# Expert layer: the first 128 of 512 tokens by gathered expert rows on VectorE, the other 384 by dense products

## Chip, cores and metric

One core of one Trainium2 chip runs one program, launched once. The metric is the device time of that program in microseconds; less is better. All times here are of the kernel before.

## What is computed

Two transformer blocks over 512 tokens of width 1024. The first block has attention in several forms and then a layer of product-key experts (`peer`); the second, twice, has other mixers and a gated MLP. Only the experts are touched:

```python
def peer(hn, w_q, subkeys, u, v):                    # 8 heads, 128 keys, top 16, 16384 experts
    q = (xt @ w_q).reshape(T, H, 2, 64)
    s = jnp.einsum('thcd,cnd->thcn', q, subkeys)
    s1, i1 = lax.top_k(s[:, :, 0], K)
    s2, i2 = lax.top_k(s[:, :, 1], K)
    cand = (s1[..., :, None] + s2[..., None, :]).reshape(T, H, K * K)
    sc, ci = lax.top_k(cand, K)
    e1 = jnp.take_along_axis(i1, ci // K, axis=-1)
    e2 = jnp.take_along_axis(i2, ci % K, axis=-1)
    idx = e1 * 128 + e2
    g = jax.nn.softmax(sc, axis=-1)
    a = jnp.einsum('cd,chkd->chk', xc, u[ic])        # for each chunk of tokens
    act = jax.nn.gelu(a) * gc
    return jnp.einsum('chk,chkd->cd', act, v[ic])
```

Each token takes 8 x 16 = 128 of 16384 experts, each a row of 1024 numbers in `u` and in `v`.

## The kernel before

All activations lie transposed: 128 features on the partitions, 8 such chunks, 512 tokens along the free dimension. The experts run dense: all 16384 hidden values of every token are computed, and those not chosen get weight 0. Expert (i, j) is row j of chunk i, so 128 chunks of 128 experts stand for all.

Products are made from halves: every fp32 operand is split into a rounded high part (fp32r) and the rest (low part), and each product is three matmuls, high x high, high x low, low x high. `Stream` brings the weights in pieces of 128x1024 (512 KiB), the same for all stages: `load` on SP's queue into 4 raw buffers, `high` on ScalarE (L363) and `low` on VectorE (L371) into 3 buffers each; `high` of piece n waits until TensorE has used piece n - 3 (`used`). The order on each engine's queue is that of the program text, and engines meet by semaphores.

The experts have four stages, one after the other:

- `queries`: the normalised tokens (h_hi, h_lo) and the queries.
- `expert_choice`, 48 steps. In each, TensorE computes one chunk of `a` (`Hidden.product`, L399: 8 feature chunks x 3 matmuls with 512 columns), ScalarE takes its gelu (L407), SP stores it to memory (`a_dram`). Beside it VectorE chooses for four tiles of 128 tokens: the 16 best of 128 keys for each of 16 half-heads (`sixteen`: max, match_replace and max_index of 8 at a time), all 256 sums of a head, the 16 best of those, then the names of the experts by comparisons with a range. The `low` splits have to be put between these operations by hand: `Pace` counts estimated us and lets one `low` through every 4.5.
- `expert_weights`, 80 steps, the other 80 chunks of `a`, 512 tokens in quads of 4. For each token ScalarE builds a one-hot row of the first key (L648, L651), VectorE two weighted rows of the second (L674, the share's high and low part), and TensorE multiplies them (L705, 256 columns), giving the token's 128x128 weights in two halves; VectorE adds the halves out of PSUM (`take`, L685) into `built`, which SP stores in tiles of 64 tokens (4 MiB). 128 quads are spread over the first 72 steps.
- `expert_outputs`, 128 steps. SP loads the `v` piece, a chunk of hidden values (256 KiB) and, for 4 chunks at once, the weights (1 MiB in rows of 1 KiB). VectorE multiplies them (`weigh`, L812), ScalarE and VectorE split the product (L792, L818), and TensorE accumulates 8 x 3 matmuls of 512 columns (L847) in all eight PSUM banks through the whole stage. `Angles` prepares tables for the second block on VectorE and ScalarE. At the end VectorE adds the banks to x (L836).

The two loops that set TensorE's work in the last two stages:

```python
for k in range(DC):                                       # L394, product of a chunk
    hi, lo = hi_w[:, k * P:(k + 1) * P], lo_w[:, k * P:(k + 1) * P]
    for m, (a, b) in enumerate(((hi, self.h_hi), (hi, self.h_lo), (lo, self.h_hi))):
        mm = self.nc.tensor.matmul(self.ps[n % 2], a, b[:, k, :], ...)
```

GpSimd does nothing in these stages, and no transfer in the kernel is issued from its queue.

## Time and profile before

| | |
|---|---|
| median of 3 runs | 4273.8 us (4264.1 to 4284.9) |
| profiled execution, its span | 4269.6 us |
| TensorE busy | 4059.4 us, 95% |
| VectorE busy | 2362.1 us, 55% |
| ScalarE busy | 1504.6 us, 35% |
| GpSimd busy | 85.6 us, 2% |
| moved by DMA | 497.2 MB, 116 GB/s on average |

The profiled execution's own time is known by its span, from its first to its last instruction; the median of the runs is 4.2 us above it. PE is TensorE's matmuls and PEld its weight loads, DVE VectorE, ACT ScalarE, POOL GpSimd, SP the engine that issues the transfers. Busy times are of instructions from start to end; matmuls overlap in the pipeline, so the pace of matmuls is read from their starts, not from their durations. The names of tiles are those of the program, with the stage before them (`outputs_prod`); `experts_ps` is PSUM in all expert stages.

### The profile page before, as it was taken

To read this page: it belongs to the slowest core of one execution; us is meant where nothing else is said; L and a number is where in the kernel's file an instruction comes from. 1 tells how busy PE (TensorE), PEld (TensorE's weight loads), DVE (VectorE), ACT (ScalarE), POOL (GpSimd) and SP (SyncE) were. 2 spreads that over 40 slices of the span, in tenths; PEclk is the share of its full clock that TensorE was granted. 3 is DMA by queue.
4 is the path that set the end of the run, shared out by engine and by line. 5 is a ranking of instruction groups with operands and counts; after the bars stand their busy time and mean duration, and the time that the engine had idled before them with its cause. 6 is when DMAs were issued, how large, how long until landed. Compare 5 with 4: busy or idle time off the path is not lost. (4 is left out here: it accounts for less than half of the span.)

```text
span 4269.6 us, 47277 instructions
## 1 busy us (share of the span) xinstructions
PE 4059.4 (95%) x18056; PEld 3239.5 (76%) x18056; DVE 2362.1 (55%) x4095; ACT 1504.6 (35%) x2600; POOL 85.6 (2%) x65
## 2 busy tenths in 40 slices
PE   8999999999999999999999998899998998998998
PEld 6667777788888878888887766777886766776886
DVE  3454445799899954544444356555434346565433
ACT  3222324233777742322222322333222232243221
POOL 0010000000000000000000001000000001000000
PEclk9988899999999999999999989999999989999999
DMA  3211113344555566666663222332332322242332
GB/s 125 77 60 30 38 40 116 100 141 133 165 205 190 177 245 196 190 193 188 189 195 101 85 69 70 95 125 84 94 90 74 97 60 72 77 148 74 94 89 69
DMA packets 183363, 497.15 MB, mean 116 GB/s; under 512 B 17826, under 2 KB 51268, under 8 KB 182116
## 3 DMA queue, kind: packets, MB, share of 16 engines
q1 hardware_dynamic: 183140, 494.14, 36.7%
q8 instruction: 145, 2.38, 0.2%
q14 instruction: 78, 0.64, 0.1%
HBM read 407.56 MB, written 85.98 MB: 116 GB/s over the span
## 5 line engine op out<-in xcount | busy, mean ns | idle before, releaser
L371 DVE TENSOR_TENSOR stream_lo<-stream_raw,stream_hi 128x1024 fp32r<-128x1024 f32 (+1 forms) x615 | 745.6, 1212 | 748.5 <-ACT stream_hi L363 747.1
L363 ACT ACTIVATE stream_hi<-stream_raw 128x1024 fp32r<-128x1024 f32 (+1 forms) x615 | 642.8, 1046 | 1430.5 <-PE experts_ps L847 492.0
L847 PE MATMUL experts_ps<-outputs_a_hi,stream_lo 128*128 128x512 f32 x1024 | 404.2, 395 | 0.0
L399 PE MATMUL experts_ps<-h_hi,stream_hi 128*128 128x512 f32 x1024 | 402.1, 393 | 1.5 <-PEq L100 1.5
L847 PE MATMUL experts_ps<-outputs_a_hi,stream_hi 128*128 128x512 f32 x1024 | 398.3, 389 | 4.2 <-DVE outputs_a_lo L818 4.2
L399 PE MATMUL experts_ps<-h_hi,stream_lo 128*128 128x512 f32 x1024 | 402.3, 393 | 0.0
L847 PE MATMUL experts_ps<-outputs_a_lo,stream_hi 128*128 128x512 f32 x1024 | 402.1, 393 | 0.0
L399 PE MATMUL experts_ps<-h_lo,stream_hi 128*128 128x512 f32 x1024 | 401.8, 392 | 0.0
L2334 PE MATMUL ffn_ps<-h_hi,stream_hi 128*128 128x512 f32 x704 | 287.4, 408 | 25.3 <-DVE h_lo L2371 25.3
L2334 PE MATMUL mid_ps<-h_hi,stream_hi 128*128 128x512 f32 x672 | 288.2, 429 | 24.0 <-DVE h_lo L2371 20.8
L2336 PE MATMUL ffn_ps<-h_hi,stream_lo 128*128 128x512 f32 x704 | 279.4, 397 | 0.0
L2335 PE MATMUL ffn_ps<-h_lo,stream_hi 128*128 128x512 f32 x704 | 279.4, 397 | 0.0
L2335 PE MATMUL mid_ps<-h_lo,stream_hi 128*128 128x512 f32 x672 | 271.1, 403 | 0.0
L2336 PE MATMUL mid_ps<-h_hi,stream_lo 128*128 128x512 f32 x672 | 270.3, 402 | 0.0
L847 PEld LDWEIGHTS experts_ps<-outputs_a_hi,stream_hi 128*128 128x128 f32 x1024 | 192.6, 188 | 47.5 <-issue 4.6
L847 PEld LDWEIGHTS experts_ps<-outputs_a_lo,stream_hi 128*128 128x128 f32 x1024 | 192.7, 188 | 45.1
L399 PEld LDWEIGHTS experts_ps<-h_hi,stream_lo 128*128 128x128 f32 x1024 | 192.9, 188 | 41.7
L399 PEld LDWEIGHTS experts_ps<-h_hi,stream_hi 128*128 128x128 f32 x1024 | 193.1, 189 | 41.4 <-issue 2.0
L399 PEld LDWEIGHTS experts_ps<-h_lo,stream_hi 128*128 128x128 f32 x1024 | 193.0, 188 | 39.6
L847 PEld LDWEIGHTS experts_ps<-outputs_a_hi,stream_lo 128*128 128x128 f32 x1024 | 193.1, 189 | 38.4
L674 DVE SCALAR_TENSOR_TENSOR weights_hot<-shared_sb,chosen,weights_g 128x256 fp32r<-128x256 f32 x512 | 208.5, 478 | 0.0
L407 ACT ACTIVATE experts_gelu<-experts_ps 128x512 f32<-128x512 f32 x128 | 76.5, 598 | 309.8 <-PE experts_ps L399 309.8
(439 smaller groups left out, 7146.3 us busy)
## 6 DMA issues: line engine op xcount, KB each, us to landing
stream_raw<-u SPq DMA_DIRECT2D x128, 512.0 KB, 3.9
stream_raw<-v SPq DMA_DIRECT2D x128, 512.0 KB, 4.1
stream_raw<-l_gu SPq DMA_DIRECT2D x88, 512.0 KB, 3.5
expert_hidden<-experts_gelu SPq DMA_DIRECT2D x128, 256.0 KB, 4.2
expert_weights<-built SPq DMA_DIRECT2D x8, 4096.0 KB, 14.2
built<-expert_weights SPq DMA_DIRECT2D x32, 1024.0 KB, 7.8
built<-expert_hidden SPq DMA_DIRECT2D x128, 256.0 KB, 4.1
stream_raw<-l_gate SPq DMA_DIRECT2D x48, 512.0 KB, 3.9
```

What stands on the lines that cost most here:

```text
L363: self.nc.scalar.activation(self.hi[n % self.RING][:, 0:w], self.raw[n % self.RAW][:, 0:w], ACT.Copy).then_inc(self.hi_done, 1)
L371: self.nc.vector.tensor_tensor(self.lo[n % self.RING][:, 0:w], self.raw[n % self.RAW][:, 0:w], self.hi[n % self.RING][:, 0:w].bitcast(F32) ...
L399: mm = self.nc.tensor.matmul(self.ps[n % 2], a, b[:, k, :], start=(k == 0 and m == 0), stop=(k == DC - 1 and m == 2))
L407: self.nc.scalar.activation(self.gelu[n % self.PLACES][:, :], self.ps[n % 2], ACT.Gelu_apprx_tanh).then_inc(self.gelu_done, 1)
L674: ins = V.scalar_tensor_tensor(out=hot2[quad % RING][:, k, :, :], in0=C.iota.unsqueeze(1).to_broadcast(both), scalar=chosen[:, 1, t:t + 1] ...
L847: mm = nc.tensor.matmul(ps[d], v, a[b % RING][:, :], start=(b == 0 and m == 0), stop=(b == KEYS - 1 and m == 2))
L2334: nc.tensor.matmul(out, hi, x_hi, start=first, stop=False)
L2335: nc.tensor.matmul(out, hi, x_lo, start=False, stop=False)
L2336: return nc.tensor.matmul(out, lo, x_hi, start=False, stop=last)
```

## The change

The first 128 tokens leave the dense path. `DIRECT` = 128 and `DENSE` = 384: the hidden products, the outputs' matmuls, their splits, products and stores are 384 columns wide. For tile 0 of the choice the experts' row numbers and shares stay with the tokens on the partitions (`Direct.at`, `Direct.share`). For each of a token's 128 experts (slots), GpSimd issues an indirect DMA that gathers one row of `u` for each of the 128 tokens (512 KiB) into one of 6 buffers, and VectorE computes the 128 dots in one instruction, a multiplication with its sum; after a gelu over all slots the same is done with `v`: a weighted sum, into two accumulators in turn. 36 dots lie in the weights stage, 92 dots and 128 weighted sums in the outputs, spread over 122 steps. At the end the accumulators are added, turned by eight transposes into PSUM beside the dense columns, and added to x by the same instructions as now.

The choice gets 72 steps and the weights 56. The candidates of a head are 112 instead of 256: all 16 second keys for the 4 best first keys, and 4 second keys for the other 12; the places are decoded with more bit operations (`places`). `Pace` lets a split through every 3.26. Turning a tile waits for later tiles by one, and tile 0 is not turned.

In the weights, a token's two halves are accumulated in PSUM by two matmuls of 128 columns instead of one of 256, so that a quad fits one bank (6 places instead of 3); the copy out of PSUM is made by ScalarE for even quads and by VectorE for odd ones. Weight tiles are 32 tokens wide and are loaded for 8 chunks at once. In the queries, eight transposes and two copies bring tile 0's normalised tokens onto the partitions. `Angles` runs earlier, from step 2. The host gives `u` once more, in rows.

```diff
 
-EG = 4
-WT = 64
-WTT = SEQ // WT
+DIRECT, DENSE = P, SEQ - P
+EG = 8
+WT = 32
+WTT = DENSE // WT
 GROUPS = KEYS // EG
...
 
-CHOICE_STEPS = 48
...
+        self.nc, self.u_rows, self.v_rows = nc, u_rows, v_rows
+        self.rows = [st.sb(f"rows{s}", [P, D]) for s in range(self.RING)]
+        self.tokens = st.sb("tokens", [P, D])
+        self.sums = []
+        self.at, self.share = st.sb("slot_at", [P, self.SLOTS], U32), st.sb("slot_share", [P, self.SLOTS])
+        self.dots = st.sb("slot_dots", [P, self.SLOTS])
...
+    def gather(self, pool, n):
+        source = self.u_rows if n < self.SLOTS else self.v_rows
+        if n >= self.RING:
+            pool.wait_ge(self.row_done, n - self.RING + 1)
+        j = n % self.SLOTS
+        self.nc.gpsimd.indirect_dma_start(self.rows[n % self.RING][:, :], None, source,
+                                          bass.IndirectOffsetOnAxis(ap=self.at[:, j:j + 1], axis=0)
+                                          ).then_inc(self.landed[n % self.RING], 16)
+
+    def row(self, dve, n):
+        dve.wait_ge(self.landed[n % self.RING], 16 * (n // self.RING + 1))
+        return self.rows[n % self.RING][:, :]
+
+    def dot(self, dve, j):
+        row = self.row(dve, j)
+        self.nc.vector.scalar_tensor_tensor(out=row, in0=row, scalar=1.0, in1=self.tokens[:, :], op0=ALU.mult, op1=ALU.mult,
+                                            accum_out=self.dots[:, j:j + 1]).then_inc(self.row_done, 1)
+
+    def activate(self, act):
+        act.wait_ge(self.row_done, self.SLOTS)
+        self.nc.scalar.activation(self.dots[:, :], self.dots[:, :], ACT.Gelu_apprx_tanh).then_inc(self.gelu_done, 1)
+
+    def mix(self, dve, j):
+        n, V, to, weight = self.SLOTS + j, self.nc.vector, self.sums[j % 2][:, :], self.dots[:, j:j + 1]
+        if j == 0:
+            dve.wait_ge(self.gelu_done, 1)
+            V.tensor_tensor(self.dots[:, :], self.dots[:, :], self.share[:, :], ALU.mult).then_inc(self.weight_done, 1)
+            dve.wait_ge(self.weight_done, 1)
+        row = self.row(dve, n)
+        if j < 2:
+            V.tensor_scalar(to, row, weight, None, ALU.mult).then_inc(self.row_done, 1)
+            return
+        dve.wait_ge(self.row_done, n - 1)
+        V.scalar_tensor_tensor(out=to, in0=row, scalar=weight, in1=to, op0=ALU.mult, op1=ALU.add).then_inc(self.row_done, 1)
+
+    def total(self, dve):
+        dve.wait_ge(self.row_done, 2 * self.SLOTS)
+        self.nc.vector.tensor_tensor(self.sums[0][:, :], self.sums[0][:, :], self.sums[1][:, :], ALU.add).then_inc(self.summed, 1)
...
+DOTS_EARLY = 36
...
+                def sums(first, last, width):
+                    shape = [P, HEADS, last - first, width]
+                    start = 0 if first == 0 else WIDE * TOPK
+                    to = cand[:, :, start:start + (last - first) * width].rearrange("p h (i j) -> p h i j", j=width)
+                    steps.mark(V.tensor_tensor(to, best[:, 0:HEADS, first:last].unsqueeze(3).to_broadcast(shape),
+                                               best[:, HEADS:H2, 0:width].unsqueeze(2).to_broadcast(shape), ALU.add))
+                    pace.spend(0.65)
...
                     dve.wait_ge(copied, t + 1)
-                    sixteen(H2, sc[t % 2], sc2, best, at, 0.2)
+                    sixteen(H2, sc[t % 2], sc2, best, at, 0.28)
                     V.tensor_copy(at_f[:, :, :], at[:, :, :]).then_inc(sc_free, 1)
-                    if t >= 1:
...
-                    wide = [P, HEADS, TOPK, TOPK]
-                    steps.after(V.tensor_tensor(cand[:, :, :].rearrange("p h (i j) -> p h i j", i=TOPK),
-                                                best[:, 0:HEADS, :].unsqueeze(3).to_broadcast(wide),
...
                         pace.spend(2.3)
                         steps.after(V.tensor_reduce(found_of(t, side), picked[:, :, :, :], AX_X, ALU.add))
                         pace.spend(2.3)
+                    if t == 0:
+                        V.scalar_tensor_tensor(out=direct.at[:, :], in0=found[0][:, 0, :], scalar=float(KEYS), in1=found[0][:, 1, :],
+                                               op0=ALU.mult, op1=ALU.add).then_inc(direct.named, 1)
...
         hot1 = [st.sb(f"hot1_{b}", [P, QUAD, KEYS], F32R) for b in range(RING)]
         hot2 = [st.sb(f"hot2_{b}", [P, QUAD, 2, KEYS], F32R) for b in range(RING)]
-        minus_done, g_hi_done, g_lo_done, far_done, hot1_done, hot2_done, mm_done, taken = (
-            st.sem(x) for x in ("minus_done", "g_hi_done", "g_lo_done", "far_done", "hot1_done", "hot2_done", "mm_done", "taken"))
+        minus_done, g_hi_done, g_lo_done, far_done, hot1_done, hot2_done, mm_done, taken_s, taken_v = (
...
             return range(*done)
 
+        def dots(n):
+            done = [DOTS_EARLY * (step - first) // (last - first) for step in (n, n + 1)]
...
+                def take(quad):
+                    wait_home(act, quad)
+                    act.wait_ge(mm_done, quad + 1)
+                    nc.scalar.activation(home(quad), place(quad), ACT.Copy).then_inc(taken_s, 1)
...
+                    for quad in quads(n - 1):
+                        if quad % 2 == 0:
+                            take(quad)
                     for quad in quads(n):
...
+                for n in range(Direct.RING, Direct.RING + DOTS_EARLY):
+                    direct.gather(pool, n)
 
             @block.vector
...
+                    wait_home(dve, quad)
                     dve.wait_ge(mm_done, quad + 1)
-                    V.tensor_reduce(built[tt % BUILT][:, :, at:at + QUAD].rearrange("p e t -> p t e"),
-                                    place(quad).rearrange("p t s e -> p t e s"), AX_X, ALU.add).then_inc(taken, 1)
+                    V.tensor_copy(home(quad), place(quad)).then_inc(taken_v, 1)
 
...
+                    for j in dots(n):
+                        direct.dot(dve, j)
 
             @block.tensor
...
                         for k in range(QUAD):
-                            mm = nc.tensor.matmul(place(quad)[:, k, :, :], hot1[quad % RING][:, k, :], hot2[quad % RING][:, k, :, :],
-                                                  start=True, stop=True)
+                            for part in range(2):
+                                mm = nc.tensor.matmul(place(quad)[:, k, :], hot1[quad % RING][:, k, :], hot2[quad % RING][:, k, part, :],
+                                                      start=(part == 0), stop=(part == 1))
                         mm.then_inc(mm_done, 1)
 
...
         self.w_dram, self.a_dram, self.hidden = w_dram, a_dram, hidden
-        place = flat(built[:, :, :])
+        place = built[:, :, :, :].rearrange("p b e t -> p (b e t)")
         width = WTT * EG * WT
         self.wgt = [place[:, s * width:(s + 1) * width].rearrange("p (t m) -> p t m", t=WTT) for s in range(self.W_RING)]
         rest = self.W_RING * width
-        self.a_raw = [place[:, rest + s * SEQ:rest + (s + 1) * SEQ] for s in range(self.A_RAW)]
+        self.a_raw = [place[:, rest + s * DENSE:rest + (s + 1) * DENSE] for s in range(self.A_RAW)]
         self.a_in = [st.sem(f"a_in{s}") for s in range(self.A_RAW)]
...
+    LATE = Direct.SLOTS - DOTS_EARLY
+    ROWS, SPREAD = LATE + Direct.SLOTS, KEYS - 6
...
+        def rows(b):
+            return range(*(ROWS * min(SPREAD, step) // SPREAD for step in (b, b + 1)))
+
+        gelu_at = next(b for b in range(KEYS) if LATE in rows(b))
+
...
 
+            @block.gpsimd
+            def _(pool):
+                for n in range(Direct.RING + DOTS_EARLY, 2 * Direct.SLOTS):
+                    direct.gather(pool, n)
...
-                        angles.turn(act, (b - 32) // 8)
+                    if b in (8, 16):
+                        angles.turn(act, (b - 8) // 8)
+                    if b == gelu_at:
+                        direct.activate(act)
 
...
                         low_a(b + AHEAD)
-                    if b == 24:
+                    if b == 2:
                         angles.begin(dve)
-                    if b in (28, 36):
-                        angles.reduce(dve, (b - 28) // 8)
-                dve.wait_ge(chunks.used, V0 + KEYS)
+                    if b in (4, 12):
+                        angles.reduce(dve, (b - 4) // 8)
+                    for n in rows(b):
+                        if n < LATE:
+                            direct.dot(dve, DOTS_EARLY + n)
+                        else:
+                            direct.mix(dve, n - LATE)
+                direct.total(dve)
...
                         for m, (v, a) in enumerate(((hi, a_hi), (hi, a_lo), (lo, a_hi))):
-                            mm = nc.tensor.matmul(ps[d], v, a[b % RING][:, :], start=(b == 0 and m == 0),
+                            mm = nc.tensor.matmul(ps[d][:, DIRECT:SEQ], v, a[b % RING][:, :], start=(b == 0 and m == 0),
                                                   stop=(b == KEYS - 1 and m == 2))
                     mm.then_inc(chunks.used, 1)
+                pe.wait_ge(direct.summed, 1)
+                for d in range(DC):
+                    mm = nc.tensor.transpose(ps[d][:, 0:DIRECT], direct.sums[0][:, d * P:(d + 1) * P], ident)
+                mm.then_inc(turned, 1)
 
...
     a["u"] = np.ascontiguousarray(x["peer_u"].reshape(KEYS, KEYS, DC, P).transpose(1, 3, 2, 0).reshape(KEYS, P, D))
```

## Rows read from the trace of the kernel before

**Rows 1.** The page's first part: busy us, share of the span, instructions.
```profile
PE 4059.4 (95%) x18056; PEld 3239.5 (76%) x18056; DVE 2362.1 (55%) x4095; ACT 1504.6 (35%) x2600; POOL 85.6 (2%) x65
```

**Rows 2.** Stretches: from:to, us; busy PE, PEld, DVE, ACT, POOL; PEclk, DMA share, GB/s.
```profile
799.20:1076.50 277.30, 277.30 (x1255) 227.97 (x1255) 264.19 (x879) 94.24 (x124) 0.00 (x0) 0.99 0.43 134
1076.50:1580.40 503.90, 502.32 (x2440) 422.68 (x2438) 443.25 (x722) 367.05 (x803) 0.00 (x0) 1.00 0.58 199
1580.40:2289.60 709.20, 705.00 (x3072) 578.26 (x3072) 323.41 (x405) 205.81 (x260) 0.00 (x0) 1.00 0.60 187
```

**Rows 3.** Waits in the outputs: waiting line, releaser, us, times, longest.
```profile
ACT stream_hi L363 <- PE experts_ps L847: 492.0, 127, 4.4
DVE stream_lo L371 <- ACT stream_hi L363: 374.6, 125, 4.3
```

**Rows 4.** Timeline of TensorE in the weights: start us, us, what ran.
```profile
1205.11 1.12 PE L705 MATMUL experts_ps<-weights_hot 128*128 128x256 f32 x8
1206.07 0.39 PE L399 MATMUL experts_ps<-h_hi,stream_hi 128*128 128x512 f32 x1
```

**Rows 5.** Page, costliest groups: a weight load; count, busy, mean ns.
```profile
L399 PEld LDWEIGHTS experts_ps<-h_hi,stream_hi 128*128 128x128 f32 x1024 | 193.1, 189 | 41.4 <-issue 2.0
```

**Rows 6.** Groups of VectorE in the choice : count, busy us, mean ns.
```profile
L547 DVE FIND_INDEX8 choice_at<-choice_best,choice_sc 128x8 uint32<-128x128 f32 x64 | 18.2, 284 | 0.0
...
L547 DVE FIND_INDEX8 choice_ci<-choice_top,choice_cand 128x8 uint32<-128x256 f32 x32 | 13.4, 419 | 0.0
...
L573 DVE TENSOR_TENSOR choice_cand<-choice_best 128x2048 f32<-128x2048 f32 x4 | 9.1, 2284 | 0.0
```

**Rows 7.** Timelines of VectorE, then ScalarE, over a step of the weights.
```profile
1201.03 3.24 DVE L674 SCALAR_TENSOR_TENSOR weights_hot<-shared_sb,chosen,weights_g 128x256 fp32r<-128x256 f32 x8
1204.19 1.22 DVE L371 TENSOR_TENSOR stream_lo<-stream_raw,stream_hi 128x1024 fp32r<-128x1024 f32 x1
...
1199.83 1.05 ACT L363 ACTIVATE stream_hi<-stream_raw 128x1024 fp32r<-128x1024 f32 x1
1200.78 1.27 ACT L648 ACTIVATE weights_hot<-shared_sb,weights_minus 128x128 fp32r<-128x128 f32 x4
...
1202.70 1.27 ACT L648 ACTIVATE weights_hot<-shared_sb,weights_minus 128x128 fp32r<-128x128 f32 x4
...
1205.31 0.60 ACT L407 ACTIVATE experts_gelu<-experts_ps 128x512 f32<-128x512 f32 x1 [0.59 <-PE experts_ps L399]
1205.81 1.06 ACT L363 ACTIVATE stream_hi<-stream_raw 128x1024 fp32r<-128x1024 f32 x1
```

**Rows 8.** Timeline of VectorE over a step of the outputs.
```profile
1801.81 1.23 DVE L371 TENSOR_TENSOR stream_lo<-stream_raw,stream_hi 128x1024 fp32r<-128x1024 f32 x1 [3.06 <-ACT stream_hi L363]
1802.95 0.68 DVE L818 TENSOR_TENSOR outputs_a_lo<-outputs_prod,outputs_a_hi 128x512 fp32r<-128x512 f32 x1
1803.56 0.69 DVE L812 TENSOR_TENSOR outputs_prod<-built 128x512 f32<-128x512 f32 x1
```

**Rows 9.** A transfer of the outputs, KB, us to landing; stretches; slices of weights.
```profile
stream_raw<-v SPq DMA_DIRECT2D x122, 512.0 KB, 4.0
...
10.00:15.00 5.00, 2.09 (x5) 1.75 (x6) 3.31 (x5) 3.66 (x6) 0.00 (x0) 1.00 1.02 384
15.00:18.00 3.00, 3.00 (x6) 1.69 (x6) 1.42 (x2) 2.50 (x4) 0.00 (x0) 1.00 1.01 417
...
GB/s 146 85 137 193 402 164 146 84 145 431 248 79 142 148 290 322 146 90 136 198 403 164 138 102 136 423 245 82 139 148 296 321 143 98 133 231 400 132 131 127
```

**Rows 10.** The same VectorE form alone (L2713) and beside GpSimd (L2360): mean ns.
```profile
L2713 DVE TENSOR_TENSOR m_rows<-m_rows 128x512 f32<-128x512 f32 x32 | 20.5, 684 | 0.0
...
L2360 DVE TENSOR_TENSOR m_rows<-m_rows,m_rstd 128x512 f32<-128x512 f32 x12 | 14.4, 1223 | 2.9 <-PEq L100 2.9
```

**Rows 11.** Timeline of SP's queue in the outputs: issues.
```profile
1704.19 0.33 SPq L354 DMA_DIRECT2D stream_raw<-v  x1
1704.62 1.07 SPq L747 DMA_DIRECT2D built<-expert_hidden  x1
```

176 lines of the change are left out of this document (114 added, 62 removed).

## Prediction

> **What bounds the kernel now.** I read the page first [rows 1]: TensorE is busy for 95% of the span of 4269.6 us, VectorE for 55%, ScalarE for 35%, GpSimd for 2%. The reader should not stop there, since an average says nothing of a stage. The table of stretches [rows 2] cuts out the four stages that the change touches, by the first and last instruction of each: choice (277.3 us), weights (503.9), outputs (709.2, of which 4.2 are an idle start) and the final additions. Together they are 1490.4 us without the tail. TensorE is without a gap in all of them; VectorE has 264.2 of 277.3 us of work in the choice, 443 of 504 in the weights and 323 of 709 in the outputs. In the outputs the waits confirm it [rows 3]: ScalarE waits 492.0 us for TensorE, and VectorE 374.6 us for ScalarE, which waits in its turn; TensorE itself waits once, for 4.2 us. So every expert stage goes at TensorE's pace, and a matmul saved is time saved, until another engine or the transfers come up. The sum below finds that next bound in each stage.
>
> **The price of a matmul.** The timeline of TensorE in the weights stage [rows 4]: eight matmuls of 256 columns start at 1205.11 and the next group at 1206.07, so 0.120 us each; 3072 of 512 columns in 705 us [rows 2] make 0.229. The line through both is 0.011 us plus 0.426 ns per column: 0.1745 us for the new 384 columns and 0.066 for 128. That a weight load shows 188 ns [rows 5] is no floor: the matmuls of 256 columns, each with its own load, come every 120 ns. A step of 24 matmuls falls from 5.50 to 4.19 us. The granted clock is full in these stretches [rows 2] and TensorE stays over 85% busy, so I change nothing there.
>
> **Choice: 72 steps instead of 48.** TensorE: 72 x 4.19 = 302 us, and what the stage holds beside its 48 products now, 277.3 - 1152 x 0.229 = 13.5 us (scores, turns, start): 315 us. VectorE: 24 more splits (low) at 1.14 us are +27. A search over 256 candidates takes 419 ns and over 128 keys 284 [rows 6], 1.05 ns an element; 5 such operations for each of 32 heads and tiles, 144 elements shorter, are 160 x 0.152 = -24. The sum of candidates goes from 9.1 us to four pairs of 512 and 384 elements, some 4.3: -5. New bit operations and their conversions, six or seven small instructions a tile, I put at 0.25 us each with their waits: +7. Total 264 + 5 = 269 us under 315: hidden, with some 0.4 us to spare in each step. If Pace (3.26 us between splits) puts them badly, the cover is thin, and a few us could show. The first six gathers go to an idle GpSimd and a DMA that is 43% busy.
>
> **Weights: 56 steps, 96 quads in the first 48 of them, two in each.** Durations are differences of starts in the timelines [rows 7]. ScalarE: a quad's one-hot rows take 1.92 us (1200.78 to 1202.70), two are 3.84; the split (high) 0.95; the gelu 0.50 at 512 columns and 0.39 at 384; the new copy of one quad out of PSUM, 512 elements, as the gelu, 0.50. Sum 5.68 us. VectorE: eight weighted rows 3.16 (8 in 1201.03 to 1204.19), one take 0.61, one split 1.14, and 36 dots over 56 steps at 1.14 are 0.73. Sum 5.64. TensorE: 4.19 + 16 matmuls of 128 columns, 1.05 = 5.24. Three engines within 8%, and ScalarE last: 48 x 5.68 + 8 x 4.19 = 306. For the waits between them I take 0.1 us a step, and the start 3 us: 314 us, against 503.9. VectorE's take falls from 1024 elements for each quad to 512 for every other one, which makes room for the dots.
>
> **Outputs: four claims on 128 steps.** TensorE: 3072 x 0.1745 = 536 us. VectorE: split 1.14, products and their low halves 0.61 at 512 [rows 8] and 0.47 at 384, so 2.08 x 128 = 266; then 92 dots and 128 weighted sums over 1024 elements, no row has them, priced as the split of 1024 with two inputs, 220 x 1.14 = 251; angles 9. Sum 526. These two alone would give some 545 with start and waits. The transfers are the third: V pieces 67.1 MB, hidden rows 25.2 and weights 25.2 (three quarters of now), gathers 220 x 512 KiB = 115.3. That is 233 MB, some 227 of it inside the stage, where 132 pass now at 187 GB/s and 60% busy [rows 2]. No row shows gathers; the transfer rate when the queues are full is bounded by rows. From below: 187 GB/s at 60.2% would be 311 at 100%, but this counts the first packets' latency of transfers that came singly. From above: two short stretches at the kernel's start, at a share of 1.0, ran 384 GB/s and 417 [rows 9]; slices of the weights stage reach 431. The new stage will have queues filled from two sides, so I take the nearer 384: 227 / 0.384 = 591 us. With 311 it would be 730, with 417 545, and there the two engines are the bound. So I expect the outputs to be bound by transfers, by a tenth over TensorE.
> The fourth is GpSimd, which issues a gather for every 2.7 us. No row in these stages has GpSimd at all; from below its price is nothing (six buffers, all in flight), from above it is a transfer's whole way, 4.0 us, if one starts only when the last has landed. I take nothing, because SP's queue, the nearest row, starts the next transfer 0.43 us after one that takes 4.0 us to land [rows 9, 11].
> The Trainium skill's page "DMA: Bandwidth & Descriptors", section Bandwidth, has 341 GB/s for a 1 MB transfer issued from GpSimd; taken as the rate of the whole stage it would give 227 / 0.341 = 666 us. The two stretches above show more, so the sum does not use it.
>
> **Ends.** The queries stage adds eight transposes and two copies after its last: +2 us. After the last product, the total of the sums, eight transposes and a longer wait: +3 us. The idle start of the outputs, 4.2 us (709.2 less 705.0) [rows 2], stays.
>
> **Sum.** 315 + 314 + 4.2 + 591 + 1 + 2 + 3 = 1230 against 1490.4: 260 us less. Profiled execution 4269.6 - 260 = 4009.4 us; the median of the runs is 4.2 above it (4273.8), so 4013.6, I say 4013.
>
> **The rivals.**
> - *The transfers keep up.* Then the outputs go at 545 us, and the weights perhaps at 306: 4013 - 46 - 8 = 3959. For it: slices at 417 and 431 GB/s. Against: a fifth of the bytes go in rows of 1 or 1.5 KB, while the slices at 431 carry the 4 MB stores in long rows. Chance 0.20.
> - *VectorE and GpSimd get in each other's way.* A 128x512 multiplication with both inputs in SBUF takes 684 ns alone and 1223 ns on average where GpSimd works on the odd chunks beside it [rows 10]: +0.54 us. Should each of 220 gathers cost VectorE as much, that is 119 us on its 526: 645, and with stalls 655 in the outputs; in the weights 36 x 0.54 = 19 more: 4013 + 64 + 15 = 4092. Against: those are GpSimd's own computations over whole tiles, and a gather reads only 128 numbers. The Trainium skill, page "SBUF — State Buffer", section Who interferes with whom, says that a VectorE instruction with two SBUF inputs contends with a GpSimd instruction that reads SBUF, each holding the shared port to its end; the rows agree that the two stretch each other, and no run yet shows a gather. Chance 0.13.
> - *Slow transfers*, at 311 GB/s: outputs 730, 4013 + 139 = 4152. Chance 0.12.
> - *It ends slower.* The mechanism: GpSimd's queue doesn't overlap its gathers, so that each takes issue to landing, 4.0 us [rows 9], and VectorE, which does its work in order, waits with the splits behind it. Outputs 220 x 4.0 = 880: 4013 + 289 = 4302. It decides from 852 / 220 = 3.9 us per gather on. For it: nothing in the trace of before excludes it. Against: it needs the six buffers to be of no use. Chance 0.06.
> - *Fewer columns don't make a shorter step*, the load setting the pace at 188 ns: 4.51 us a step, +23 in the choice and nothing where others bind: 4036. The 256-column rows speak against it. Chance 0.04.
>
> **How the numbers follow.** Forecast 0.45 (3985 to 4040), the rivals 0.20, 0.13, 0.12, 0.06, 0.04. The range 3952 to 4130 takes in all but the slow transfers' upper part and the slower case, some 0.17. A measurement of this kernel tells 0.5% from no change. All cases but the serial gathers are faster, by 3% (slow transfers) to 7%: faster 0.92, same 0.02, slower 0.06.
>
> **What would show it.** Right: choice 315, weights 314, outputs near 591 us; TensorE's 384-column matmuls at 0.175 us from start to start; in the outputs a DMA share over 0.95, VectorE waiting for rows or for V pieces, TensorE idle for a tenth. Wrong: a DMA share well under 0.9 with TensorE without gaps (transfers keep up); a dot longer than 1.3 us (the port); GpSimd's queue issuing at even distances of over 2.7 us with the DMA half idle (GpSimd the bound); a choice longer than 320 us (Pace). The forecast falls most easily by the dots' unseen price: each 0.1 us on 220 is 22 us on VectorE, which 65 us of slack cover in the outputs.

## The result, and the profile after the change

The changed kernel takes 4137.3 us (median of 4 runs, 4122.9 to 4145.4) against 4268.9 for the kernel before in the same series: ratio 0.968, interval 0.966 to 0.970. It is 3.2% faster. 132 us came of the 260 that were forecast, and the time lies 7 us above the range.

The profiled execution has a span of 4137.4 us. The page's first part, as [rows 1]:

```profile
PE 3791.5 (92%) x18318; PEld 3208.1 (78%) x18325; DVE 2446.6 (59%) x4301; ACT 1455.3 (35%) x2492; POOL 463.2 (11%) x321
```

The same stretches as [rows 2], with the same columns (from:to, us; busy PE, PEld, DVE, ACT, POOL; granted clock, DMA share, GB/s). They are the choice, the weights, an idle start that now deserves a line of its own, the outputs and the ends:

```profile
801.00:1116.00 315.00, 313.47 (x1834) 312.04 (x1835) 272.52 (x932) 124.18 (x173) 5.91 (x6) 0.99 0.54 175
1116.00:1440.30 324.30, 323.47 (x2112) 322.03 (x2111) 303.46 (x561) 298.97 (x643) 32.89 (x36) 1.00 0.75 261
1440.30:1452.00 11.70, 0.00 (x0) 0.03 (x1) 1.26 (x3) 0.97 (x2) 0.84 (x1) 0.61 1.05 390
1452.00:2156.00 704.00, 578.37 (x3075) 562.57 (x3076) 538.97 (x716) 193.60 (x260) 338.45 (x214) 0.90 0.89 322
2156.00:2165.00 9.00, 1.18 (x9) 0.97 (x8) 5.77 (x10) 2.04 (x4) 0.00 (x0) 0.70 0.12 48
```

Choice and weights have TensorE without a gap. The outputs don't: 704 us against 705 before, although TensorE has a quarter less to do in them. No engine is busy for more than 578 us, and the transfers for 89%. The span is 128 us above its forecast of 4009.4. Of these, 113 lie in one row, 704 where 591 was forecast; the rest is small: +7.5 in the idle start, +10.3 in the weights, 3 less in what is left.

The waits of the outputs (engine, line, what it waited for: us in total, times, longest), as [rows 3]:

```profile
ACT outputs_a_hi L931 <- DVE outputs_prod L953: 464.7, 118, 14.2
POOL experts_rows L464 <- DVE experts_rows L474: 168.3, 52, 15.8
DVE outputs_prod L953 <- DMA built<-expert_hidden: 149.1, 46, 11.3
POOL experts_rows L464 <- DVE outputs_sums L492: 142.9, 43, 12.4
PE experts_ps L994 <- DVE outputs_a_lo L959: 136.3, 29, 11.8
```

Read it from TensorE down: TensorE waits for VectorE's low half of the product, VectorE for a chunk of hidden values from memory, and ScalarE and GpSimd wait for VectorE, which does its work in order. The largest number, ScalarE's 464.7, is that of an engine with little to do; the cause is the third line. It has 46 waits, and the longest is eleven microseconds. Of the 127 steps of TensorE (from the first matmul of a chunk to that of the next), 88 take 4.2 to 4.8 us; 15 take over 7 us, up to 15.7, and hold 117 of the 166 us that all steps together are above 4.2. They come about once in eight steps, and once in eight steps SP issues the weights of 8 chunks: 1.5 MB in rows of 1 KB (L877). One such place in the timelines of SP's queue, VectorE and GpSimd:

```profile
1812.44 0.33 SPq L355 DMA_DIRECT2D stream_raw<-v  x1
1812.87 0.38 SPq L872 DMA_DIRECT2D built<-expert_hidden  x1
1813.29 0.43 SPq L877 DMA_DIRECT2D built<-expert_weights  x1
1816.90 0.33 SPq L355 DMA_DIRECT2D stream_raw<-v  x1
1817.33 4.49 SPq L872 DMA_DIRECT2D built<-expert_hidden  x1
1821.87 0.43 SPq L355 DMA_DIRECT2D stream_raw<-v  x1
...
1821.73 2.47 DVE L492 SCALAR_TENSOR_TENSOR outputs_sums<-experts_rows,experts_slot_dots,outputs_sums 128x1024 f32<-128x1024 f32 x2
1835.10 0.56 DVE L953 TENSOR_TENSOR outputs_prod<-built 128x384 f32<-128x384 f32 x1 [10.91 <-DMA built<-expert_hidden]
...
1825.40 0.93 POOL L464 DMA_INDIRECT experts_rows<-v,experts_slot_at  x1 [0.30 <-issue]
1838.73 1.01 POOL L464 DMA_INDIRECT experts_rows<-v,experts_slot_at  x1 [12.39 <-DVE outputs_sums L492]
```

The hidden values issued at 1817.33 and after have 1.5 MB and a `v` piece ahead of them in the same queue, and share the transfer engines with the gathers. The chunk issued at 1817.33 is the one that VectorE takes at 1835.10, 17.8 us later. VectorE stands for 10.91 us. Stretches cut from the same place, in the columns of [rows 2], show what the transfers do meanwhile:

```profile
1813.30:1822.00 8.70, 8.58 (x49) 8.00 (x47) 8.70 (x11) 2.96 (x4) 6.87 (x5) 1.00 0.95 295
1822.00:1828.00 6.00, 4.36 (x24) 4.04 (x24) 2.20 (x2) 0.00 (x0) 3.42 (x4) 1.00 1.05 399
1828.00:1835.10 7.10, 0.00 (x0) 0.00 (x0) 0.00 (x0) 0.00 (x0) 0.00 (x0) 0.54 1.02 395
1835.10:1843.00 7.90, 5.59 (x20) 5.62 (x21) 7.90 (x10) 2.94 (x4) 2.01 (x2) 0.55 0.65 217
```

While VectorE stands still, from 1824.2 to 1835.1, the transfers run at full rate, 395 to 399 GB/s, mostly on things that aren't wanted next (gathers for six buffers, the rest of the weights); when VectorE goes on, they fall to 0.65 and 217 GB/s, since every buffer is full and GpSimd may issue only when VectorE has used a row. So the rate at full was there. What fails is the order, and the 0.89 share is its mark. The 295 GB/s of the first stretch is not the price of the 1 KB rows: in the second, at 399 GB/s, 738 of 1152 packets are under 2 KB. TensorE stands still from 1826.4 to 1837.4; its granted clock is at the lower level (1.2 GHz) from 1828.5 to 1842.2, so through the first 4.8 us of its work afterwards.

The other steps have a limit of their own. VectorE's products start at 1810.72, 1815.19 and 1819.65: with two rows to add up, its work for a step takes 4.47 us, more than TensorE's 4.16. The median step of the stage is 4.36.

In the standstill, from 1828.0 to 1835.1, both sides have work pending and get nearly equal parts of the transfer engines (queue: packets, MB, share of 16 engines):

```profile
q0 software_dynamic: 420, 1.51, 54.1%
q1 hardware_dynamic: 590, 1.29, 47.5%
```

q1 is SP's queue, q0 that of GpSimd's gathers. The Trainium skill, page "DMA: Bandwidth & Descriptors", section SWDGE vs HWDGE vs iDMA, says that each transfer engine serves its inner queues in turn; these rows agree. What SP asks for thus goes at about half the rate while gathers are pending. From 1813.3 to 1835.1 its queue moves 3.55 MB (1.45, 0.81 and 1.29 in the three stretches), which is 163 GB/s, and that of the gathers 4.20 MB. From 1812.44 up to and with the late chunk SP asks for 3.0 MB (`v`, hidden values, weights, `v`, hidden values); at 163 GB/s that is 18 us, an estimate. A chunk of hidden values is asked for only 7.5 us before VectorE takes it (median of the stage). In the kernel before it was asked for 5.6 us ahead, and VectorE's waits for it came to 3.6 us in the whole stage, with no gathers and a DMA share of 0.60.

### The profile page after: what moved, and what is told of

It is laid out like the page before. It is cut to its first block and busy times, and to the rows that moved or that the text cites. A ratio compares the mean times of both kernels' runs of the same rounds, so it can differ in the third digit from the quotient of the medians.

```text
span 4137.4 us, 48279 instructions
## 1 busy us (share of the span) xinstructions
PE 3791.5 (92%) x18318; PEld 3208.1 (78%) x18325; DVE 2446.6 (59%) x4301; ACT 1455.3 (35%) x2492; POOL 463.2 (11%) x321
## 5 line engine op out<-in xcount | busy, mean ns | idle before, releaser
L994 PE MATMUL experts_ps<-outputs_a_hi,stream_hi 128*128 128x384 f32 x1024 | 363.7, 355 | 137.4 <-DVE outputs_a_lo L959 136.3
L994 PE MATMUL experts_ps<-outputs_a_lo,stream_hi 128*128 128x384 f32 x1024 | 357.2, 349 | 0.0
L994 PE MATMUL experts_ps<-outputs_a_hi,stream_lo 128*128 128x384 f32 x1024 | 356.6, 348 | 0.0
L400 PE MATMUL experts_ps<-h_hi,stream_hi 128*128 128x384 f32 x1024 | 348.1, 340 | 1.5 <-PEq L101 1.5
L400 PE MATMUL experts_ps<-h_hi,stream_lo 128*128 128x384 f32 x1024 | 344.8, 337 | 0.0
L400 PE MATMUL experts_ps<-h_lo,stream_hi 128*128 128x384 f32 x1024 | 344.7, 337 | 0.0
L994 PEld LDWEIGHTS experts_ps<-outputs_a_hi,stream_hi 128*128 128x128 f32 x1024 | 203.5, 199 | 153.5 <-DVE stream_lo L372 132.6
L464 POOL DMA_INDIRECT experts_rows<-u_rows,experts_slot_at x128 | 162.1, 1267 | 1295.6 <-DVE experts_rows L474 674.3
L931 ACT ACTIVATE outputs_a_hi<-outputs_prod 128x384 fp32r<-128x384 f32 x128 | 67.2, 525 | 502.0 <-DVE outputs_prod L953 474.7
L464 POOL DMA_INDIRECT experts_rows<-v,experts_slot_at x128 | 216.0, 1687 | 183.9 <-DVE outputs_sums L492 142.9
```

Source lines behind the costliest of these rows:

```text
L400: mm = self.nc.tensor.matmul(self.ps[n % 2], a, b[:, k, :], start=(k == 0 and m == 0), stop=(k == DC - 1 and m == 2))
L464: self.nc.gpsimd.indirect_dma_start(self.rows[n % self.RING][:, :], None, source, bass.IndirectOffsetOnAxis(ap=self.at[:, j:j + 1], axis=0 ...
L931: nc.scalar.activation(a_hi[b % RING][:, :], prod[b % 2][:, :], ACT.Copy).then_inc(a_hi_done, 1)
L994: mm = nc.tensor.matmul(ps[d][:, DIRECT:SEQ], v, a[b % RING][:, :], start=(b == 0 and m == 0), stop=(b == KEYS - 1 and m == 2))
```

## Experiments

In all of them the outputs are measured from TensorE's first product to its last, the gap is TensorE's idle time before them, and long steps are those over 7 us with their sum above 4.2. The kernel before took 4271.0 to 4272.4 us (medians) beside them. Three theories are named in the expectations: QUEUE, the big transfer makes what stands behind it late; RATE, the sum of bytes sets the stage; PORT, VectorE and GpSimd stretch each other.

| kernel | whole, us | ratio to before | outputs | long steps | gap |
|---|---|---|---|---|---|
| the change | 4137.3 | 0.968 [0.966, 0.970] | 703.9 | 15, 117 us | 11.8 |
| w_spread | 4095.4 | 0.9585 [0.956, 0.961] | 657.9 | 11, 42 | 12.1 |
| w_on_act | 4094.6 | 0.9586 [0.956, 0.961] | 657.7 | 10, 44 | 12.2 |
| no_gathers | 3984.3, one run | | 566.0 | 1 | 3.7 |
| no_row_math | 4101.6, one run | | 669.0 | 14, 103 | 10.2 |
| deep_a | 4047.9 | 0.9488 [0.947, 0.951] | 609.1 | 7, 36 | 12.0 |
| spread_deep | 4044.1 | 0.9465 [0.945, 0.948] | 616.5 | 7, 43 | 12.0 |
| spread_dots | 4065.2 | 0.9516 [0.950, 0.953] | 629.2 | 8, 29 | 12.3 |
| dots_end_early | 4135.9, one run | | 703.3 | 15, 116 | 3.8 |
| all_candidates | 4143.1 | 0.9697 [0.968, 0.972] | 700.3 | 16, 115 | 12.2 |
| columns_64 | 4138.3, one run | | 703.9 | 15, 121 | 11.9 |
| combined | 4012.1 | 0.9377 [0.935, 0.940] | 584.0 | 6, 30 | 4.0 |
| combined_more | 4013.5 | 0.9390 [0.937, 0.941] | 567.2 | 3, 11 | 5.2 |

**The burst on SP's queue: spread, or moved to another queue.** `w_spread` loads the same weights in four parts in four steps; `w_on_act` leaves the transfer whole and issues it from ScalarE.

```diff
-                    if b % EG == EG - 1 and b // EG + W_RING < GROUPS:
-                        weighing.load_w(sp, b // EG + W_RING)
+                    g, k = (b - EG + 1) // EG, (b - EG + 1) % EG
+                    if b >= EG - 1 and k < 4 and g + W_RING < GROUPS:
+                        weighing.load_part(sp, g + W_RING, k)          # w_spread: 3 of the 12 tiles of tokens
...
                         high_a(b + AHEAD)
+                    if b % EG == EG - 1 and b // EG + W_RING < GROUPS:
+                        weighing.load_w(act, b // EG + W_RING)         # w_on_act
```

> The changed kernel, with each weights load of the outputs (1.5 MB, once in 8 steps) cut into four of 384 KB that SP issues in four successive steps, between the loads of V pieces and hidden rows. Theory QUEUE: in the changed kernel one step of eight takes 10 to 15 us instead of 4.2, because the hidden rows and V pieces behind the 1.5 MB on the same queue come late while gathers take turns with its 1 KB rows. Then the long steps go, and the outputs fall from 704 us to 625 to 640 (227 MB at 364 GB/s, the rate of the stage divided by its share of busy transfers), the total from 4137 to about 4065. Theory RATE: the transfers as a whole bound the stage, whatever their order: the outputs stay at 690 to 704 us and the total within 10 us of 4137. Theory PORT (VectorE and GpSimd stretch each other): no change either.

> The changed kernel, with the weights loads of the outputs issued whole (1.5 MB) from ScalarE's queue instead of SP's. QUEUE in its first form (order in one queue): V pieces and hidden rows no longer stand behind them, the long steps go, the outputs take 625 to 640 us. If it is the burst on the 16 engines that holds all others back, and not the order in the queue, the long steps stay, perhaps shorter: 660 to 704. RATE: 690 to 704. ScalarE waits for nothing new, since the products it would wait for are older than those its own split waits for.

Both take 42 us off the whole and 46 off the outputs, and in `w_spread` the longest step falls from 15.7 to 9.2 us. Both edits take the burst out of the way of the small transfers in SP's queue, and `w_on_act` leaves its size and its 1 KB rows as they were. So 46 us are the burst's place in that queue. But 658 is over the 625 to 640 expected of QUEUE, and the long steps didn't go: 10 or 11 are left, with 42 to 44 us. Waits and stretch of `w_spread`:

```profile
DVE outputs_prod L961 <- DMA built<-expert_hidden: 105.3, 63, 5.1
...
1451.50:2108.00 656.50, 574.77 (x3065) 552.43 (x3066) 540.01 (x716) 193.07 (x260) 329.06 (x214) 0.96 0.95 345
```

The waits for hidden values are shorter, more in number and still there; the share is 0.95. These rows can be read as a stage at its bytes or as one whose small transfers still come late. The next but one experiment parts the two.

**Is it the gathers, or VectorE's work on them?** `no_gathers` issues only the first six gathers and computes all dots and sums on their buffers again (the other 250 gathers are left out, 131 MB). `no_row_math` gathers everything and computes dots and sums over 8 of 1024 elements.

```diff
         if n >= self.RING:
-            pool.wait_ge(self.row_done, n - self.RING + 1)
+            return                                                     # no_gathers
...
-        self.nc.vector.scalar_tensor_tensor(out=row, in0=row, scalar=1.0, in1=self.tokens[:, :],
+        row = row[:, 0:8]                                              # no_row_math
+        self.nc.vector.scalar_tensor_tensor(out=row, in0=row, scalar=1.0, in1=self.tokens[:, 0:8],
```

> The changed kernel without all gathers but the first six: VectorE makes the same 256 row instructions over the rows of those six (the scale in the dots is 0.1 so that numbers stay small). It leaves out 128 MB of transfers and GpSimd's work. QUEUE and RATE: outputs at the pace of TensorE and VectorE, 545 to 555 us, no long steps. PORT: the same, but VectorE's row instructions would get shorter than 1.22 and 1.28 us. If VectorE's order or its work were the cause, the outputs stay over 600. The idle time between weights and outputs, 11.8 us in the changed kernel against the 4.2 of before, falls back to about 4 if it waits for the last gather.

> The changed kernel with all gathers, but the dots and weighted sums over 8 of the 1024 elements of each row, so that VectorE loses some 1.0 us for each of 256 rows (the first two weighted sums stay whole). QUEUE: the outputs keep their long steps and take 650 to 700 us, since the transfers are all there. RATE: 690 to 704. If VectorE's load were the bound, the outputs fall to 545. PORT: GpSimd's gather instructions, 0.93 us at best and 1.3 to 1.7 on average beside a full VectorE, would all come near 0.93.

Without the gathers, with the burst and with all of VectorE's work, one long step is left and the outputs take 566 us, 11 over the 545 to 555 expected. With VectorE's row work cut down, 14 of 15 long steps stay, and the outputs take 669, as QUEUE had it. So the long steps need the gathers and not VectorE's load. Cutting that load brings 35 us: 14 in the long steps (117 to 103), the rest in the others; the median of all steps falls from 4.36 to 4.16. PORT falls for VectorE: a dot takes 1218 ns with a range of 21 in the changed kernel and 1220 without the gathers, a weighted sum 1276 and 1277. It holds the other way round. GpSimd's issues (duration ns min/median/max), first in the changed kernel, then in `no_row_math`:

```profile
L464 POOL DMA_INDIRECT experts_rows<-u_rows,experts_slot_at x128: 933/1305/1898, 878.2 to 1726.4; - x128
L464 POOL DMA_INDIRECT experts_rows<-v,experts_slot_at x128: 933/1298/3814, 1728.8 to 2126.6; - x128
...
L474 DVE SCALAR_TENSOR_TENSOR experts_rows<-experts_rows,experts_tokens x128: 1206/1218/1227, 1128.2 to 1749.5; 128x1024 f32<-128x1024 f32 x128
```

```profile
L464 POOL DMA_INDIRECT experts_rows<-u_rows,experts_slot_at x128: 933/937/1949, 878.3 to 1705.0; - x128
L464 POOL DMA_INDIRECT experts_rows<-v,experts_slot_at x128: 932/937/2762, 1706.6 to 2086.5; - x128
```

An issue takes 0.94 us where VectorE's row instructions are short and 1.3 beside the full ones. GpSimd was busy for 338 of 704 us, so this cost nothing that these runs show.

**More hidden values in hand.** `deep_a` keeps the burst where it was and gives the chunks of hidden values 8 buffers instead of 4. It tells two theories apart that `w_spread` left together: if the bytes set the stage, buffers can't help.

```diff
+        deep = 2 * self.A_RAW
...
-        if b >= self.A_RAW:
-            sp.wait_ge(self.prod_done, b - self.A_RAW + 1)
-        sp.dma_start(self.a_raw[b % self.A_RAW], self.a_dram[b]).then_inc(self.a_in[b % self.A_RAW], 16)
+        if b >= deep:
+            sp.wait_ge(self.prod_done, b - deep + 1)
+        sp.dma_start(self.a_raw[b % deep], self.a_dram[b]).then_inc(self.a_in[b % deep], 16)
...
+        weighing.a_raw += [st.sb(f"a_raw{s}", [P, DENSE])[:, :] for s in range(weighing.A_RAW)]
```

> The changed kernel with 8 buffers instead of 4 for the chunks of hidden values that the outputs load; the weights still come in one transfer of 1.5 MB every 8 steps. In the changed kernel VectorE's waits in the outputs are for these hidden values (149 us in 46 waits, the longest 11.3). QUEUE-A (the big transfer makes the next hidden values late, and these alone make the step late): with 8 in hand they are there, the long steps (excess 117 us) fall to under 40 us, the outputs take 625 to 660 us instead of 704, the whole 4060 to 4095. QUEUE-V (whatever stands behind the 1.5 MB in SP's queue is late, and the v piece is next, because SP issues both in order): VectorE's or TensorE's wait moves to the v piece, the long steps stay, outputs 690 to 705, the whole 4120 to 4137. RATE (the transfers' average sets the stage): outputs not under 227 MB at 345 to 364 GB/s, that is 623 to 658 us, in either case.

> Weights in four parts (as in w_spread: outputs 658 us, whole 4095) and also 8 buffers for the hidden values. RATE: w_spread already ran at 347 GB/s with the engines of the DMA busy for 0.9 or more of nearly all slices, so more buffers bring little: outputs 645 to 660 us, whole 4085 to 4098. QUEUE: w_spread still waited 105 us in 63 waits for hidden values, and these are what is left: outputs 600 to 630 us, whole 4040 to 4070.

The outputs fall from 704 to 609 us and the whole by 89, more than any theory had; the long steps go down to 7 with 36 us, as QUEUE-A had it. The waits of `deep_a` in the outputs, and its outputs as a stretch:

```profile
ACT outputs_a_hi L935 <- DVE outputs_prod L957: 222.1, 96, 7.6
ACT stream_hi L364 <- DMA stream_raw<-v: 144.8, 43, 10.9
...
DVE stream_lo L372 <- ACT stream_hi L364: 65.4, 18, 9.3
PEld experts_ps L998 <- DVE stream_lo L372: 50.8, 15, 7.6
PE experts_ps L998 <- DVE outputs_a_lo L963: 46.4, 15, 7.3
...
1440.40:2049.50 609.10, 562.34 (x3075) 553.80 (x3076) 536.07 (x716) 197.33 (x260) 347.90 (x214) 0.95 0.99 372
```

VectorE's waits for hidden values are gone from the list, and TensorE waits 46.4 us, not 136.3. QUEUE-A names the cause, though its 625 to 660 us was too high. RATE, as it was named, is wrong: 345 to 364 GB/s had been taken for the limit from runs in which late hidden values held the gathers back. What is left is what QUEUE-V named: the 7 long steps go with 6 waits of VectorE for ScalarE's split (3.8 to 9.3 us), and ScalarE waited for a `v` piece. Stretches around one of them, with the weights issued at 1597.05 and VectorE standing from 1615.7 to 1625.0:

```profile
1603.00:1612.00 9.00, 9.00 (x54) 9.00 (x53) 9.00 (x17) 2.95 (x4) 6.25 (x5) 1.00 1.05 389
1612.00:1626.00 14.00, 7.74 (x45) 7.42 (x43) 4.70 (x9) 2.27 (x4) 3.15 (x3) 0.86 1.03 396
1626.00:1640.00 14.00, 13.15 (x62) 13.18 (x63) 14.00 (x24) 5.21 (x7) 8.81 (x6) 0.78 0.88 294
```

The weights pass at 389 to 396 GB/s here too, and the slow stretch comes after the wait. So a mean share of 0.99 is near the limit but not at it: full stretches here show 1.03 to 1.05. The stage's 226 MB at 396 GB/s would be 572 us, an estimate.

With `spread_deep`, expected at 600 to 630 by QUEUE and at 645 to 660 by RATE, the outputs take 616.5: with 8 buffers, spreading the burst brings nothing more (the wholes' intervals overlap). Its 7 long steps are all at the first chunk of a new set of weights, so there the weights themselves seem to be late; the profile doesn't name that wait.

**Fewer bytes in the outputs.** `spread_dots` is `w_spread` with 24 of the 92 dots put into the choice, one after every second split from tile 1 on.

```diff
             self.chunks.low(self.dve, self.next)
             self.next += 1
+            if self.direct is not None and self.next % 2 == 0 and self.dot < DOTS_CHOICE:
+                self.direct.dot(self.dve, self.dot)
+                self.dot += 1
+                self.spent += 1.3
```

> Weights in four parts (as in w_spread) and 24 of the 92 dots of the outputs moved into the choice, one after every second split from tile 1 on, with their gathers: 12.6 MB leave the outputs and 24 x 1.3 = 31 us of VectorE. VectorE in the choice rises from 272 to about 304 us of 315. RATE: the outputs fall by 12.6 MB at 345 GB/s = 36 us, from 658 to 620 us, the whole to 4060 (4050 to 4075). QUEUE (the stage waits for the order in SP's queue, not for the sum of bytes): outputs stay at 645 to 660, whole 4080 to 4095. If the choice, which has only 11 us left on VectorE, becomes late, it shows as choice over 318 us and the whole is up to 20 us more than either.

29 of the 36 us came, and the whole, 4065.2, lies in RATE's range; VectorE's 297 us in the choice stayed under TensorE's 315. The edit takes 24 dots of VectorE's work out of the outputs together with their bytes, so it doesn't show which of the two brought the 29 us.

**The gap before the outputs.** `dots_end_early` spreads the 36 dots of the weights stage over its first 52 steps instead of 56.

```diff
-            done = [DOTS_EARLY * (step - first) // (last - first) for step in (n, n + 1)]
+            done = [DOTS_EARLY * min(step - first, last - first - 4) // (last - first - 4) for step in (n, n + 1)]
```

> The changed kernel with the 36 dots of the weights stage spread over its first 52 steps instead of 56, so that the last gather of that stage is issued four steps (17 us) before its end. In the changed kernel TensorE stands still for 11.8 us between the last hidden product and the first product of the outputs; without gathers it was 3.7. If the stage's end waits for the last gather's landing (issued at 1440.20 there, with the next stage's first work at 1450.05), the gap falls to 3.5 to 5 us and the whole by 7 to 8 us, to 4130. If the gap comes from elsewhere (the first weights and hidden values of the outputs not yet loaded, the start of the stage itself), it stays at 10 to 12.

The last gather of the weights stage and VectorE's first work of the outputs, in the changed kernel and then in `dots_end_early` (start us, us, what ran, idle before):

```profile
1440.20 0.94 POOL L464 DMA_INDIRECT experts_rows<-u_rows,experts_slot_at  x1 [3.22 <-DVE experts_rows L474]
...
1450.15 0.56 DVE L953 TENSOR_TENSOR outputs_prod<-built 128x384 f32<-128x384 f32 x1 [10.22 <-PEq L101]
```

```profile
1427.03 0.94 POOL L464 DMA_INDIRECT experts_rows<-u_rows,experts_slot_at  x1 [3.23 <-DVE experts_rows L474]
...
1445.67 0.56 DVE L953 TENSOR_TENSOR outputs_prod<-built 128x384 f32<-128x384 f32 x1 [3.42 <-PEq L101]
...
1447.52 0.66 PE L994 MATMUL experts_ps<-outputs_a_hi,stream_hi 128*128 128x384 f32 x1 [3.84 <-DVE outputs_a_lo L959]
1447.98 0.53 PE L994 MATMUL experts_ps<-outputs_a_lo,stream_hi 128*128 128x384 f32 x1
1448.30 0.53 PE L994 MATMUL experts_ps<-outputs_a_hi,stream_lo 128*128 128x384 f32 x1
```

The gap is 3.8 us as expected, against 11.8. `no_gathers`, which computes its dots up to the stage's end, has 3.7. So the 8 us were the wait, at the stage's end, for a gather issued in its last step, and not for a dot. The span of this one execution is only 3 us shorter: what comes before the experts' first product is 1.9 us longer in it, choice and weights 1.6, and what comes after the outputs 1.9. One execution can't tell this from scatter. The last two lines show TensorE's lower clock after the gap (0.5 granted from 1446.4 to 1453.2): a matmul of 384 columns every 0.32 us, where the full clock has 0.1745.

**The matmuls of the weights stage.** Here the forecast was 10 us short, and the timeline of the changed kernel shows the term:

```profile
1253.77 2.04 PE L829 MATMUL experts_ps<-weights_hot 128*128 128x128 f32 x16
1255.64 0.39 PE L400 MATMUL experts_ps<-h_hi,stream_hi 128*128 128x384 f32 x1
```

Sixteen matmuls of 128 columns take 1.87 us, 0.117 each, not 0.066; those of 256 took 0.120 [rows 4]. `columns_64` makes them 64 columns wide: the high part's product goes to one half of a token's place, the low part's to the other, and the sum of the two is left out.

```diff
-    mm = nc.tensor.matmul(place(quad)[:, k, :], hot1[quad % RING][:, k, :], hot2[quad % RING][:, k, part, :],
-                          start=(part == 0), stop=(part == 1))
+    half = slice(64 * part, 64 * part + 64)
+    mm = nc.tensor.matmul(place(quad)[:, k, half], hot1[quad % RING][:, k, :],
+                          hot2[quad % RING][:, k, part, half], start=True, stop=True)
```

> The changed kernel with the 768 matmuls of the weights stage cut from 128 to 64 columns each (the high part writes the first half of a token's place, the low part the second; the sum of the two parts is left out). The changed kernel's matmuls there come every 0.117 us, where a line through 256 and 512 columns gave 0.066, and one of 256 columns takes 0.120. FLOOR (below some 256 columns a matmul with its own weight load doesn't come faster): still 0.115 to 0.120 us each, the weights stage stays at 322 to 325 us. WIDTH (each has a fixed cost of its own and still a cost by column, 128 columns being dear for another reason such as the accumulation of two in one place): 0.06 to 0.10 us, the stage 305 to 318 us, where ScalarE's 5.7 us a step binds.

```profile
1253.01 1.98 PE L830 MATMUL experts_ps<-weights_hot 128*128 128x64 f32 x16
1254.83 0.42 PE L400 MATMUL experts_ps<-h_hi,stream_hi 128*128 128x384 f32 x1
```

1.82 us for sixteen, 0.114 each, and the stage as long as it was: FLOOR. Between 64 and 256 columns the width costs 6 ns. What sets the floor, the weight load or something else, was not tried.

**The shorter candidate list.** `all_candidates` searches all 256 sums of a head again, in the changed kernel.

```diff
-    CAND = WIDE * TOPK + (TOPK - WIDE) * NARROW
+    CAND = TOPK * TOPK
...
-                    sums(0, WIDE, TOPK)
-                    sums(WIDE, TOPK, NARROW)
+                    sums(0, TOPK, TOPK)
```

> The changed kernel with all 256 candidates of a head in the choice instead of 112, and with the two bit operations for their places instead of five. HIDDEN (the choice goes at TensorE's pace, 72 steps of 4.2 us): VectorE rises in the choice from 272.5 us by 24 (160 searches of 144 elements more) and 5, less 7 for the bit operations, to 290 to 298 of 315 us; the choice stays 315 to 317 us and the whole at 4137 (4128 to 4146). THIN (the cover of VectorE is too thin once the splits wait behind longer stretches of choice): choice 320 to 330 us, the whole 4142 to 4152.

VectorE rose to 290.6 us in the choice's stretch, as expected. From the first hidden product to the first product of the weights it took 323.3 us instead of 319.1, 4.2 more: between the 0 to 2 more of HIDDEN and the 5 to 15 of THIN. The whole is 6 us longer with overlapping intervals. So the 112 candidates bring some 4 us in the trace, and no difference that the times can tell.

**Together.** `combined` is `deep_a` with 24 dots in the choice and the weights stage's dots ending early; `combined_more` moves ten more dots out of the outputs, and its dots in the weights stage end three steps early.

```diff
-DOTS_EARLY = 36
+DOTS_CHOICE = 24                          # combined_more: 28
+DOTS_EARLY = 36 + DOTS_CHOICE             # combined_more: 42 + DOTS_CHOICE
```

> The changed kernel with three of the edits together: 8 buffers for hidden values in the outputs, 24 dots moved into the choice, and the dots of the weights stage ending four steps before its end; the weights still in one transfer of 1.5 MB. RATE (with 8 buffers the outputs go by the sum of bytes): deep_a moved 227 MB in 609 us, 373 GB/s; 12.6 MB less is 34 us less, 575 us, and with 8 us from the idle start the whole is 4048 - 42 = 4006 (3998 to 4015). REST (what deep_a has left are long steps after the big transfer, 36 us in 7 steps, which don't go by the sum of bytes): outputs 590 to 609, the whole 4020 to 4040.

> As combined, with 28 dots in the choice and 42 in the weights stage, so 10 dots and 5.2 MB fewer in the outputs. The choice's VectorE comes to 272 + 36 = 308 of 315 us, that of the weights stage to 310 of 324. RATE: outputs 14 us less than combined, whole 3985 to 4003. TensorE's own 536 us plus start are then nearer, so the gain may be less than 14. If one of the two stages grows because its VectorE has no more room, it shows in its span: choice over 318 or weights over 327, and the whole equals combined or is up to 15 us above it.

The choice, the weights, the gap and the outputs of `combined`:

```profile
801.00:1116.00 315.00, 313.47 (x1839) 312.04 (x1839) 298.04 (x982) 124.28 (x174) 35.80 (x30) 1.00 0.70 215
1116.00:1440.00 324.00, 321.45 (x2105) 319.32 (x2103) 302.78 (x560) 298.29 (x640) 33.67 (x36) 1.00 0.78 265
1440.00:1443.60 3.60, 0.00 (x0) 0.00 (x0) 1.12 (x3) 0.83 (x2) 0.00 (x0) 1.00 1.08 374
1443.60:2027.50 583.90, 547.81 (x3072) 540.80 (x3073) 508.85 (x668) 197.69 (x260) 314.40 (x190) 0.97 0.99 369
```

4012.1 us, 6.2% under the kernel before and 3.0% under the changed one. The share is 0.99 at 369 GB/s, and 24 dots with their 12.6 MB took 25 us off the outputs of `deep_a`. The whole lies in RATE's range, the outputs (584) between RATE's 575 and REST's 590, with 6 long steps left. Here too bytes and VectorE's work went together. `combined_more` shows where this ends. Its outputs fall by another 17 us to 567, but its choice, with VectorE at 306.5 of 330 us, becomes 11 us longer (330.0 instead of 319.1 from product to product), and nothing is won. The last branch of the expectation named this: choice over 318 us, the whole as in `combined` or up to 15 us above.

## Why the prediction failed, by its steps

**Right: the price of a matmul at 384 columns, and the choice.** Undisturbed steps take 4.16 us against 4.19, the choice 315 against 315, VectorE in it 272.5 against 269. TensorE's work in the outputs at that price is 536 us; the 578 of the table hold the matmuls at the lower clock after each standstill. The rival that fewer columns make no shorter step is out.

**Wrong in size: the matmuls of 128 columns.** The step "the line through both" (0.011 us plus 0.426 ns per column) was drawn from 256 and 512 columns and used at 128. With 0.117 instead of 0.066, TensorE has 4.19 + 1.87 = 6.06 us in a step with two quads, more than ScalarE's 5.68: 48 x 6.06 + 8 x 4.19 = 324.4, which is the 324.3 measured (steps with two quads take 6.04 us). TensorE bound this stage, not ScalarE.

**Wrong in part: the idle start.** "The idle start of the outputs, 4.2 us, stays" looked at engines and not at what a stage has to wait for at its end. A gather issued in the last step made it 11.7.

**Right that transfers bind, wrong in how: the outputs.** The step was 227 MB / 384 GB/s = 591 us, as if a stage bound by its transfers had them busy all the time. Its bytes were right (226.4 MB passed) and its rate was not the fault: 395 to 399 GB/s in the rows above at full share, and 372 over the whole stage in `deep_a`, which gives 609. So of the 113 us, 95 are the order and the shallow buffers, as `deep_a` measures: 1.5 MB, a `v` piece and the gathers ahead of 192 KB that VectorE wants within 7.5 us. The other 18 are the step from 384 to 372 GB/s. `deep_a` runs at 389 to 400 in full stretches and still has 36 us in long steps, so they too look like waits, and not like a limit of the rate; no edit parts them. The profile of before had the means to see it: SP issues everything of the stage from one queue in the order of the text, and the change made the weights' transfer 1.5 MB in every eighth step where it was 1 MB in every fourth, and put the gathers beside it. I added bytes and never asked which transfer waits behind which, and how many steps ahead it is asked for. The sentence on what would show the prediction wrong named a share well under 0.9 and TensorE without gaps; what came was 0.89 with gaps, which none of the rivals had. It had VectorE wait for rows or for V pieces; not one dot or weighted sum of the changed kernel waited for its row, and the late transfer was the one that the prediction doesn't name, the hidden values.

**Too low: the two engines alone.** The prediction gives them 545 us. `no_gathers` has all their work and takes 566. VectorE's row instructions start every 1.195 us (two from 1808.33 to 1810.72), not every 1.14, and its busy time in the outputs is 539 us against 526 forecast. The sum also holds a term of 1 us that no sentence of the prediction names.

**The rivals.** *Slow transfers*, 4152 us, is nearest to the time and wrong in its reason: the mean of 322 GB/s resembles its 311, but it is a mean over stalls. *VectorE and GpSimd in each other's way*: the dots took 1218 ns and the weighted sums 1276, with ranges of 21 and 17 ns, and as long without the gathers. The Trainium skill's rule (page "SBUF — State Buffer", section Who interferes with whom) held in this case for one of the two: GpSimd's issue was stretched from 937 to 1305 ns, VectorE not at all. The 341 GB/s of its page "DMA: Bandwidth & Descriptors", section Bandwidth, lies under the full rate of 395 to 399 seen here; a sum with it would have given 666 for the outputs, an estimate between the 704 of the change and the 609 of `deep_a`, so right for neither. *Serial gathers* fell: 220 in 704 us with GpSimd waiting 311 us for VectorE to free a buffer. *Transfers keep up* fell: the outputs take 609 us in `deep_a` with the transfers busy for 0.99, not 545, and even without gathers 566.

**Settled and open.** That four buffers of hidden values instead of eight cost the outputs 95 us is shown by an edit that changes nothing else. What is left in `deep_a`, 609 against 536 of TensorE, goes down when dots leave the stage (`combined`, `combined_more`), with their bytes and VectorE's work at once. How it divides into bytes, VectorE's work, the waits for `v` pieces and the clock after them was not taken apart.

## What to carry to other kernels

When a change adds transfers, adding up bytes gives the floor of a stage only; for each small transfer that an in-order engine waits for, ask what is ahead of it on its queue, how the queues share the engines, and how long before its use it is issued. A share of 0.9 with long single waits can be a sign of order, and the remedy may be more buffers for the smallest tile (here 6 KB on each partition) rather than fewer bytes. With that mended, look for the next late transfer: here it was the `v` piece. And a line through two widths of a matmul held between them here (at 384), not below them.
